# Extra transposes ahead of the projections of a fused two-block transformer kernel

## What is computed

```
def swiglu(h, w_in, w_out):
    a, b = jnp.split(h @ w_in, 2, axis=-1)          # 1024 -> 2 x 2816
    return (jax.nn.silu(a) * b) @ w_out             # 2816 -> 1024

for l in range(2):
    mx = (silu(c) @ ada_w[l] + ada_b[l])            # 9 vectors of 1024; mc the same for the context
    x    = x    + 0.5 * mx[2] * swiglu(ada_norm(x, ...),    ffn_w_in[l, 0], ffn_w_out[l, 0])
    hctx = hctx + 0.5 * mc[2] * swiglu(ada_norm(hctx, ...), ffn_w_in[l, 0], ffn_w_out[l, 0])
    ...                                             # mixer l
    x = x + 0.5 * mx[8] * swiglu(ada_norm(x, ...), ffn_w_in[l, 1], ffn_w_out[l, 1])
    ...                                             # hctx too, in layer 0 alone
```

## Time and profile before

| | |
|---|---|
| Median of three runs | 2336.16 us (2329.62, 2336.16, 2337.82) |
| The profiled execution's own time | 2331.44 us |
| Its span | 2329.7 us |
| PE, weight loads, DVE, ACT, POOL busy | 96%, 90%, 49%, 36%, 8% |
| Matmuls | 19336 |
| Mean granted TensorE clock | 0.98 |

### The profile page before, as it was taken

One profiled execution on the slowest core, in us unless ns is written; L12 is line 12 of the kernel. 1 busy time (PEld: TensorE's weight loads), 2 busy tenths in 40 slices (PEclk: granted clock), 3 DMA queues, 4 the chain that ended last, 5 costly groups with the idle time before them and its releaser, 6 DMA issues.

```text
span 2329.7 us, 47012 instructions
## 1 busy us (share of the span) xinstructions
PE 2238.8 (96%) x19336; PEld 2096.1 (90%) x19336; DVE 1145.8 (49%) x1926; ACT 847.7 (36%) x1383; POOL 176.5 (8%) x150
## 2 busy tenths in 40 slices
PE   6999999999999999988999999999999999998998
PEld 4986798789999999976999999999999998978998
DVE  5226365653333345457563433454343446477665
ACT  4125444731222233238432222243122234355444
POOL 0003112100000010401200000010000010001000
PEclk8999999999999999999999999999999998999999
DMA  9654454355575344430354666242233233224573
GB/s 308 184 162 124 145 149 112 109 155 163 170 211 164 112 138 121 137 91 28 100 156 152 191 208 189 81 129 83 81 108 99 86 96 95 77 82 123 173 212 115
DMA packets 515900, 315.76 MB, mean 136 GB/s; under 512 B 16035, under 2 KB 513274, under 8 KB 515622
## 3 DMA queue, kind: packets, MB, share of 16 engines
q1 hardware_dynamic: 515160, 313.45, 45.6%
q10 hardware_dynamic: 590, 0.16, 0.0%
HBM read 312.50 MB, written 1.06 MB: 135 GB/s over the span
## 4 chain that ended last, share of the span: by engine, by line
PE 89%; DVE 6%; ACT 2%; DMA 1%; issue 1%; ACTq 0%; SPq 0%; POOL 0%; DVEq 0%; POOLq 0%
PE ps L1080 66%; PE ps L1124 4%; PE ps L813 3%; PE ps L1027 3%; PE ps L997 2%; DVE w_lo L1905 1%; PE ps L955 1%; PE ps L2159 1%; PE ps L2175 1%; ACT w_hi L1428 1%; PE ps L886 1%; PE ps L2523 1%; PE ps L2198 1%; DMA stage<-in_ffn_w_in 1%; PE ps L2427 0%
## 5 line engine op out<-in xcount | busy, mean ns | idle before, releaser
L1080 PE MATMUL ps<-h_hi,w_hi 128*128 128x256 f32 x3424 | 739.9, 281 | 8.1 <-issue 3.6
L1080 PE MATMUL ps<-h_lo,w_hi 128*128 128x256 f32 x3424 | 732.4, 279 | 0.0
L1080 PE MATMUL ps<-h_hi,w_lo 128*128 128x256 f32 x3424 | 731.9, 279 | 0.0
L1080 PEld LDWEIGHTS ps<-h_hi,w_hi 128*128 128x128 f32 x3424 | 548.6, 190 | 27.9 <-issue 26.4
L1080 PEld LDWEIGHTS ps<-h_lo,w_hi 128*128 128x128 f32 x3424 | 548.8, 190 | 0.1
L1080 PEld LDWEIGHTS ps<-h_hi,w_lo 128*128 128x128 f32 x3424 | 547.7, 189 | 0.0
L1905 DVE TENSOR_TENSOR w_lo<-stage,w_hi 128x1024 fp32r<-128x1024 f32 x227 | 285.2, 1259 | 440.9 <-ACT w_hi L1428 440.3
L1428 ACT ACTIVATE w_hi<-stage 128x1024 fp32r<-128x1024 f32 x227 | 236.8, 1056 | 338.7 <-PE ps L1080 207.2
L1905 DVE TENSOR_TENSOR w_lo<-deep,w_hi 128x1024 fp32r<-128x1024 f32 x184 | 226.2, 1234 | 227.8 <-ACT w_hi L1428 226.5
L1428 ACT ACTIVATE w_hi<-deep 128x1024 fp32r<-128x1024 f32 x184 | 192.0, 1056 | 177.2 <-PE ps L1080 138.1
L1080 PE MATMUL ps<-g_hi,w_hi 128*128 128x256 f32 x1100 | 230.5, 278 | 0.2
(11 more groups left out here) (405 smaller groups left out, 2831.5 us busy)
## 6 DMA issues: line engine op xcount, KB each, us to landing
modw<-in_ada_w SPq DMA_DIRECT2D x72, 1024.0 KB, 6.8
stage<-in_ffn_w_in SPq DMA_DIRECT2D x88, 512.0 KB, 3.9
deep<-in_ffn_w_in SPq DMA_DIRECT2D x88, 512.0 KB, 4.0
modw<-in_w_mod SPq DMA_DIRECT2D x18, 1024.0 KB, 7.9
stage<-in_w_in SPq DMA_DIRECT2D x30, 512.0 KB, 5.1
stage<-in_ffn_w_out SPq DMA_DIRECT2D x32, 384.0 KB, 3.5
stage<-in_even_w_in SPq DMA_DIRECT2D x24, 512.0 KB, 4.1
deep<-in_ffn_w_out SPq DMA_DIRECT2D x32, 384.0 KB, 3.5
```

The lines of the kernel that those rows point to most:

```text
L1080: last = mm(ps[:, j, v - a:v - a + SEQ], w_part[wp][:, u % RING, c, :], x_part[xp][:, x, v:v + SEQ], start=first and wp == xp and v == a, ...
```

## The change

Three edits, all in PE's program:

1. `settle`, a new function in `pe_gemm`: two transposes of `modr` into bank 6, the same as in `pe_cols`, whose result nobody reads. A chained projection issues it ahead of its first segment pair, after a wait for `mod_kept` (bank 6 must have been read).
2. A projection that has the new key `settle` (A, B and C of the feed-forward (1, 0)) issues it once, after the first two units of an up projection or the first unit of a down projection. PE's turns are written out there as straight code, in place of the hardware loop.
3. A token projection into `vtok` issues it once, after its first tile of 24 matmuls.

```diff
--- before.py
+++ after.py
@@ -267,23 +267,24 @@
                              "sg_half": 4, "gh_hi": 4, "g_half": 2, "g_ready": 2}, w=w)
             elif (l, i) == (1, 1):
                 norm("pre", nt, block=1, l=l, n=2 * i)
+            settle = (l, i) == (1, 0)
             for half in range(2):
                 if half == 0 and (l, i) != (1, 1):
-                    gemm(w, 2 * P, 2 * FH - 4, "swiglu", tok=(0, nt), dst=2, hper=hpers[0])
+                    gemm(w, 2 * P, 2 * FH - 4, "swiglu", tok=(0, nt), dst=2, hper=hpers[0], settle=settle)
                     if (l, i) == (0, 0):
                         modvec(1, 0, (0,), (1,))
                 elif nt == SEQ:
                     gemm(w, half * FH * P, 4, "swiglu", tok=(0, nt), dst=0)
                     gemm(w, half * FH * P + 2 * P, 2 * FH - 4, "swiglu", tok=(0, nt), dst=2, paired=False)
                 else:
-                    gemm(w, half * FH * P, 2 * FH, "swiglu", tok=(0, nt), dst=0, hper=hpers[2 * half])
+                    gemm(w, half * FH * P, 2 * FH, "swiglu", tok=(0, nt), dst=0, hper=hpers[2 * half], settle=settle)
                 w_down = dict(w=("ffn_w_out_2", l, i), src="g", ks=(6, 5), row0=half * FH, l=l, g=2 * i)
                 if half and after:
                     gemm(w_down.pop("w"), 0, KC - 2, "resid", tok=(0, nt), sumsq="early", **w_down)
                     after(dict(w=("ffn_w_out_2", l, i), **w_down))
                 else:
                     gemm(w_down.pop("w"), 0, KC, "resid", tok=(0, nt), sumsq="resid" if half else None,
-                         fed=not (last and i and half), peel=i and half, hper=hpers[2 * half + 1], **w_down)
+                         fed=not (last and i and half), peel=i and half, hper=hpers[2 * half + 1], settle=settle, **w_down)
 
         w = ("even_w_in_2", 0) if l == 0 else ("odd_w_in_2", 0)
 
@@ -1067,6 +1068,11 @@
             def weights(i, u):
                 eng.wait_ge(S("w_ready"), i * (step * per) + (u + 1))
 
+            def settle():
+
+                for c in range(2):
+                    tr(ps[:, 6, c * P:(c + 1) * P], modr[:, 0, c * P:(c + 1) * P], ident)
+
             order = k["order"]
             memory_after = {1: (0, 1), 2: (2,), 3: (3,)} if k["w"] == ("even_w_out_2", 0) else {}
 
@@ -1123,6 +1129,8 @@
                         for wp, xp in W_X:
                             last = mm(ps[:, bank, (tile % 2) * SEQ:(tile % 2) * SEQ + SEQ], x_part[xp][:, c, tile * P:(tile + 1) * P],
                                       w_part[wp][:, u % RING:u % RING + 2, c, :], start=c == 0 and wp == xp, stop=c == KC - 1 and wp == "lo")
+                    if k["dst"] == "vtok" and j + tile == 0:
+                        settle()
                 up(last, "unit_done", rounds, by=2)
 
             def pair_rows(i, pair, rounds):
@@ -1130,8 +1138,14 @@
                     pe_rows(eng, p, i, k["hper"], x, rounds)
 
             if chained(p):
+                eng.wait_ge(S("mod_kept"), p.at("mod_kept"))
+                settle()
                 pair_rows(0, 0, 1)
-            for i, js, rounds in turns(eng, k["n"], step, apart=chained(p)):
+            if k.get("settle"):
+                order_of_turns = [(i, range(min(step, k["n"] - i * step)), 1) for i in range(-(-k["n"] // step))]
+            else:
+                order_of_turns = turns(eng, k["n"], step, apart=chained(p))
+            for i, js, rounds in order_of_turns:
                 paired = k.get("paired", True) and evac != "tok" and per == 1 and len(js) >= 2 and ("pairs" not in k or i < k["pairs"])
                 for j in js:
                     segments = () if chained(p) else twins(p, j, js)
@@ -1153,6 +1167,8 @@
                             pair_rows(i, pair + 1, rounds)
                         elif rounds > 1 or i < k["n"] // step - 1:
                             pair_rows(i + 1, 0, rounds)
+                    if k.get("settle") and (i, j) == (0, 2 - per):
+                        settle()
                     if "extra" in k:
                         pe_extra(eng, p, j)
```

## The result

The changed kernel takes 2335.47 us (median of 20 runs, 2330.31 to 2347.23), the kernel before 2329.94 us (median of 20, 2325.43 to 2342.87). The ratio is 1.0026, 95% interval 1.0014 to 1.0038: some 6 us slower, under the 0.5% that was set as the bound, and inside the range of 2329 to 2347. The 20 runs of before put its median 6 us lower than the three that were shown.

What follows compares the result with a forecast made beforehand. TensorE, busy 96%, bounds the kernel through its matmul pace. Gains and costs sum to +5.5 us on 2331.44 (2337.0); from the median, 2336.16 + 5.5 - 4.2 gives 2337.5 us, range 2329 to 2347.

Steps and rivals of the forecast that it cites:

- The wait in front of C: Layer 0, both C's (second half up): segment matmuls wait for DVE's reduction, 2.25 and 3.2 us late, 5.5 us in all.
- The bound with both late: Layer 0's C's: upper bound of the wait cost if both were as late as the second, 6.4 us.
- The fall of the clock: Behind the idle time at both C's: one short fall each, 2 x 1.7 = 3.4 us lost; ends 0 and 6.8.
- Layer 0's pairs: Before A, B and C: gains 0.83 (first A), 0.56 and 0.57 us (B's), sum 1.96; cost 0.9 where nothing is awaited.
- Layer 1: First feed-forward: A's other 768 matmuls turn short, 3.4 us gained; B and C already short; three pairs cost 0.7 us.
- Written-out code at nothing: Layer 1's first feed-forward: 1608 more matmuls of straight code cost nothing; other end 2.8 us for 13 more fetches.
- The rival in which it misses: Layer 1's pairs land on the long pace; A gains nothing, B, C and D become long: 2348.9 us, chance 0.08.
- The token projections: Into vtok: two pairs cost 0.4 us and gain nothing, the form being bound to the long pace; otherwise 2.3 us gained.
- the pace has nothing to do with transposes: Rival for all new pairs: nothing is gained, 2342.9 us, chance 0.08.
- the clock stayed up: Rival at layer 0's C's: no fall behind the waits, 2334.1 us, chance 0.2; with short token projections 2331.8, chance 0.1.
- the waits were hidden: Rival: waits at C hidden and earlier runs at the long pace all through layer 1: 2324.3 us, chance 0.04.
- the pair in C brings back 4.2 us: Layer 1's C: in runs where it is long, its pair turns 960 matmuls short, 4.2 us gained.

Runs made afterwards that it cites:

- The second execution: The changed kernel, unedited, profiled a second time; waits of 1.69 and 2.99 us at the two C's; no whole-kernel time given.
- the first experiment: Changed kernel without the wait and the pair in front of both C's of layer 0: 0.999 of the kernel before, median 2334.69 us.
- the same five pairs: Against the changed kernel, pairs only at layer 0's A's and B's and in layer 1's A: 0.9981 and 0.9965; with D pairs added 1.0016.

## Why the prediction was right, and where its terms were off

**The wait in front of C** was the largest term and was right in kind: PE waits for DVE's reduction at both C's, nowhere else, and it is not made up later. It was put at 5.5 us. From B's last transposes to C, before and after differ by 4.55 us in the first feed-forward (2.17 us from the transposes to C's first matmul before, 6.72 after), and by 5.6 in the second (up to its second turn's transposes: 24.06 and 29.65). The first has 1.7 us of the clock in it, the second 1.7 and the 0.8 of the long turn. So the waits cost 2.85 and 3.1 us, 6.0 against 5.5, and waits and clock 9.4 us against 8.9. The term that was too low is the first feed-forward's (2.25): idle 2.46 us against 1.8, because the weight split ahead of the evacuation, which waits for a landing, was nearly as late as in the second one. There the estimate of 3.2 us met 3.1, and 2.8 us of idle time met 2.73. The bound with both late (6.4 us) was the better guess. The 0.8 us of a C that is long behind its pair was in no term: the forecast had layer 0's C's short as before.

**The fall of the clock**: 1.7 us at each place was predicted and measured. The second execution had one fall and the kernel with the wait alone lost 3.4 us behind its idle time of 4.24 us, so the ends of 0 and 3.4 a place are both real. The kernel without the wait has neither idle time nor fall.

**Layer 0's pairs**: 0.83, 0.56 and 0.57 us predicted and measured (by the chain 21.98, 15.18 and 15.18 now), for 0.22 us a pair. B's gain is firm: 15.65 us without a pair in all 12 cases of six profiles, 15.09 with one in all 16 of eight. A's is not: without a pair, five of six profiles have the first feed-forward's first turn long, the sixth short; and with the pairs, A's second turn was long instead in six of 16 cases (22.72 us), five of them in the second feed-forward, where the first turn was short in four of six profiles without any pair. Without a pair the second turns were never long. So in the second feed-forward one of A's turns was long in five of eight profiles with the pair and in two of six without.

**Layer 1**: -3.4 + 0.7 us predicted, 281.54 us before and 11.31 + 0.22 + 87.06 + 0.05 + 7.74 + 0.22 + 63.28 + 0.22 + 108.81 = 278.91 after: -2.6. Written-out code at nothing: right. (The straight code that was its cover is at 113.3 ns from start to start, not 112.9: 280 matmuls have 279 steps.) That the pair acts on A: six of seven profiled executions with it have A's 768 short, in one of them A was short already, and none of six without a transpose there has. The rival in which it misses came true once for A, and B stayed long behind its pair in two profiles, but C turned short behind its pair in both.

**The token projections**: no gain was right, 0.2 us of cost instead of 0.4. The reason given, that this form is bound to the long pace, fell: one execution ran it short. What is shown is only that no pair moved it, neither the 16 of the kernel with one behind every tile nor the two of the changed kernel.

**The rivals.** That the pace has nothing to do with transposes is refuted by the counts: B's first turns in layer 0 (none of 12 short without a pair, 16 of 16 with one) and layer 1's A. The section of the Trainium skill named there ("TensorE: Matmul & The Clock Gate", section "Back-to-back issue gap") gives 262 cycles for 256 columns, 109 ns at 2.4 GHz, as the gap of isolated matmuls, and says that in a stream of weight loads and matmuls both set the spacing. It is thus no statement on how many paces such a stream has; the profiles here have two, both above 109 ns. Read as a price, the same page's figure of about 275 ns for a bf16 transpose in the section "Part 4: PE-mode transpose" isn't met by the float32 ones here: a pair costs 0.22 us in the chain. As the time of one from start to end it nearly is (median 272 ns over the 22 new ones). The other rivals: the clock stayed up at one of the four waits of the changed kernel's two profiles, and the waits were hidden at none.

**The sum**: +5.5 us predicted for the profiled execution, +5.4 in the span. By stages it is 10.1 (9.4 and the long turn's 0.8, rounded) - 1.96 + 0.9 - 2.6 + 0.2 = +6.6, and the first D, long in this execution and short in that of before, adds 2.0; stages that the change doesn't touch took back the rest. So the near agreement of the span is partly luck, while the ratio over 20 runs, 6.1 us, lies near the sum. The 2.0 us between 2337.5 and the measured median are two errors that nearly cancel, which is luck: the three runs of before stood 6.2 us over the median of the 20, and the step "the pair in C brings back 4.2 us" took 4.2 off. For the kernel before that step has no support: C ran short in both its profiles. The mechanism exists, though: in two profiles (the changed kernel's second, and the first experiment) C began long and its pair turned it short. There B was long before it, which no profile of the kernel before has.

**What stays open**: what decides the pace. It holds over hundreds of matmuls, it can change at the start of a projection, one or two transposes change it in some places and not in others, and in executions of the same code the D's come out long or short, all three together in 13 of 14 profiles. No run here tells what in PE keeps it. Nor do the times of whole kernels settle what the pair in layer 1's A is worth: three timings of kernels with the same five pairs gave 0.9965, 0.9981 and, with pairs in the D's, 1.0016.

## What to carry to other kernels

A cheap extra instruction on the bounding engine costs what it waits for, not what it does: the two transposes took 0.22 us each time, and the wait that two of the six places in layer 0 needed cost 9.4 us with the clock's fall, against some 5.3 us gained in layer 0's other four (1.96) and in layer 1 (2.6 and its three pairs' 0.7). Look at who last used the bank, and leave the edit out where that use is just before, above all where the state that it aims at is there already. And when a gain is a pace that differs between executions of one code, take several profiles before counting on it, and compare the stages that the edit doesn't touch as well.

## What the runs showed of the hardware

- Two paces of the same 128x128 by 128x256 matmul at a granted clock of 1.00: 113.4 and 117.9 ns from one to the next, with PE and weight loads busy throughout. Stages that no edit touched differed between executions by it: 792 matmuls of the last feed-forward took 89.76 or 93.28 us.
- Behind one or two transposes inside layer 1's A and C, an up projection went from long to short in eight of nine cases (768 matmuls in 87.3 us instead of 90.6); behind two ordinary matmuls, tried once, it didn't. Behind a pair inside layer 1's B and the D's, a down projection at the long pace stayed long in all five cases.
- Idle times of PE of 2.46, 2.73, 2.99 and 3.08 us, each after dense matmuls, were followed by 3.4 us at 1.2 GHz, one of 4.24 us by 6.8 us, and one of 1.69 us by none.
